# A convolutional streaming encoder layer: weight sums in the place of their first terms, a ring of five blocks, a second C22 buffer, a reordered last pair, and filler matmuls at the start

## The chip, the cores and the metric

The kernel runs on one core of a Trainium2 chip. The metric is the device time of one launch in microseconds (us). Engines are named as the profile names them: PE is TensorE (PEld its weight loads), DVE is VectorE, ACT is ScalarE, POOL is GpSimd, SP is SyncE, which here only issues transfers.

## What is computed

One layer of a chunk-causal streaming encoder on 1088 frames (1024 of a new stream, 64 of running ones), with model width 1024, DA = DB = 512 and DF = 2816. Cut to what matters:

```python
h = rms_norm(x, norm1_g)
z = h @ w_in                                   # 1024 x 4608
a_val, a_gate, b_g, c_g, b_val, gates = split(z)
u = a_val * sigmoid(a_gate)
u = silu(layer_norm(causal_dwconv31(u) + b_dw_a)) ; y_a = u @ w_a_out
v = causal_dwconv3(c_g * b_val)                   ; y_b = (b_g * v) @ w_b_out
x = x + (sigmoid(g_a) * y_a + sigmoid(g_b) * y_b) @ w_o
h = rms_norm(x, norm2_g)
f_gate, f_val = split(h @ w_up)                # 1024 x 5632
x = x + (silu(causal_dwconv3(f_gate)) * f_val) @ w_down
y = rms_norm(x, final_g)                       # and the new conv states
```

## The kernel before

**Products.** Every fp32 product is made of three matmuls in a faster number format: an operand is split into a high part and a remainder, and high x high, high x low and low x high are added (function `three`, L368 to L371). A matmul has 128 partitions and 272 columns. The two wide projections (`w_in`, `w_up`) run as a 2 x 2 scheme with seven products instead of eight. One application of it is a *job*: it makes 2 x 128 output channels for all frames (or, for half jobs, half of the frames). There are 43 jobs, j0 to j42: j0 to j5 the value and gate of mixer A (j0 to j3 are half jobs), j6 to j11 mixer B, j12 to j19 the merge gates ("S" jobs, whose results are spilled to HBM, 544 KB twice a job), j20 to j42 the up projection of the ConvFFN (j20 and j21 half jobs). Each of the seven products of a job takes one weight block of 128 x 512, and 24 matmuls (12 in a half job). In order the blocks are A11, S1, S2, S4, S3, A12, A22. A11, A12, A22 are pieces of the matrix as they are ("plain" here), and S1 to S4 are sums of pieces. Product *s* of a job is called slot *s*.

**Order on PE.** j0 to j19, then P1 (8 blocks of `w_b_out`), P2 (8 blocks of `w_a_out`), WO (32 blocks of `w_o`), j20 to j22, then ten pairs of ConvFFN channels: a job ("E"), a down projection D (4 blocks of `w_down`, 48 matmuls each), and a job ("O"). The last down projection and the transposes of the output follow. The program of each engine is written out by hand in this order.

**A block's way.** All 393 blocks are numbered. Block n comes by a transfer from SP, ACT rounds it into `w_hi` (function `hi`, L749), DVE makes the remainder `w_lo` (function `lo`, L1115), and PE uses it in product n. `w_hi` and `w_lo` have RING = 4 places, and in slot b of a job ACT and DVE handle block b + LOOK with LOOK = 3. The blocks of a job arrive in a staging tile `stg` of eight places, from which DVE makes the four sums (function `weight_sum`, L1168 to L1179) a job ahead, one in each of slots 1 to 4. Their loads wait for older blocks to be through (semaphores `wlo`, `sums`). The blocks of P1, P2, WO and D ("direct") are loaded into `w_raw`, which is the memory of `w_lo`, so their load waits until the product that used the place is done (`used`).

**Other work.** In a slot, ACT first copies results of earlier products out of the accumulator banks BA, BB, BC, BS (function `copies`), then does `hi`. DVE combines these results (the C22 half goes through `ss_w` or `ss_f`), and works on the 31 taps of mixer A's convolution (L1297, 1.38 us each, 120 of them), spread over the jobs j2 to j19. POOL adds up `e_b` over channels in three additions. After j19, DVE subtracts the mean from `cv`, and then splits `bv` into `qb_hi` and `qb_lo`, for which P1 waits. At the very end, j42 is followed by its split `q_lo`, for which the last down projection waits, since D of the pair before comes ahead of j42.

## Time and profile before

| | us |
|---|---|
| median of 3 runs (1561.3 to 1563.38) | 1561.84 |
| the profiled execution's own time | 1564.04 |
| its span | 1561.1 |
| PE busy | 1403.1 (90%) |
| DVE busy | 1111.0 (71%) |
| ACT busy | 525.4 (34%) |
| POOL busy | 79.5 (5%) |

The span is that of one profiled execution, and the times of the trace below are measured from its start. Its own time is the device time of the same execution, 2.94 us more than its span, and 2.2 us above the median. "Busy" is the time in which an engine had an instruction under way, which for PE includes stretches at the lower of its two clocks.

### The profile page before, as it was taken

Reading aid. Unit: us, or ns where it says so; the run is one execution under the profiler, and the core shown is the slowest. Engines: PE = TensorE matmul, PEld = TensorE weight load, DVE = VectorE, ACT = ScalarE, POOL = GpSimd, SP = SyncE. Lnnn points to the kernel's source line nnn. Section 1 sums busy time; section 2 is a strip of 40 time slices with the busy share of each in tenths; the row PEclk is TensorE's granted clock in tenths of the full one; section 3 lists DMA queues with packets and bytes.
Section 4 is the critical chain, followed back from the end, with each engine's and each line's share of the span. In section 5 each row is a group of like instructions: output and inputs, shape, how many; then the busy total and the mean of one; then the engine's idle time right before and its main releaser. Section 6 shows DMA issues by size and latency. Waiting matters only on the chain.

```text
span 1561.1 us, 25790 instructions
## 1 busy us (share of the span) xinstructions
PE 1403.1 (90%) x10658; PEld 1369.0 (88%) x10658; DVE 1111.0 (71%) x1622; ACT 525.4 (34%) x854; POOL 79.5 (5%) x88
## 2 busy tenths in 40 slices
PE   4799999899996899997989999999999999999967
PEld 2699999898986899986889898999999898989967
DVE  5989999998865443467776667676667766676745
ACT  6743322333433333345422222323222222223122
POOL 2000000000000042211000000000000000000001
PEclk9999999999998899988899999999999999999988
DMA  5121111122214353321111111111121111111013
GB/s 167 49 74 48 48 55 48 63 83 98 99 65 147 112 180 106 89 61 48 55 47 42 48 35 55 41 42 55 31 64 35 48 41 48 35 55 35 27 41 116
DMA packets 137659, 102.98 MB, mean 66 GB/s; under 512 B 5389, under 2 KB 130055, under 8 KB 137543
## 3 DMA queue, kind: packets, MB, share of 16 engines
q1 hardware_dynamic: 134716, 92.21, 19.5%
q10 hardware_dynamic: 2827, 9.13, 1.5%
q8 instruction: 84, 1.38, 0.4%
q14 instruction: 32, 0.26, 0.1%
HBM read 87.77 MB, written 13.55 MB: 65 GB/s over the span
## 4 chain that ended last, share of the span: by engine, by line
PE 46%; DVE 28%; issue 10%; ACT 8%; DMA 6%; POOL 1%; ACTq 0%; SPq 0%; DVEq 0%
DVE cv L1297 6%; PE BA L369 5%; PE BC L369 5%; PE BA L371 5%; PE BA L370 5%; PE BC L371 5%; PE BC L370 5%; DMA w_raw<-in_w_down 4%; DVE cvf L1532 4%; DVE w_lo L1115 4%; ACT w_hi L749 3%; PE BB L369 3%; PE BB L370 3%; PE BB L371 3%; PE BS L369 2%
## 5 line engine op out<-in xcount | busy, mean ns | idle before, releaser
L1115 DVE TENSOR_TENSOR w_lo<-stg,w_hi 128x512 fp32r<-128x512 f32 x301 | 214.4, 714 | 130.5 <-ACT w_hi L749 129.6
L749 ACT ACTIVATE w_hi<-stg 128x512 fp32r<-128x512 f32 x301 | 187.9, 626 | 292.2 <-PE BA L371 91.3
L369 PE MATMUL BB<-hb,w_hi 128*128 128x272 f32 x788 | 233.1, 296 | 35.1 <-ACT ss_f L831 22.6
L369 PE MATMUL BA<-hb,w_hi 128*128 128x272 f32 x812 | 238.7, 294 | 23.9 <-DVE t_out L1195 8.1
L370 PE MATMUL BA<-hb,w_hi 128*128 128x272 f32 x812 | 235.7, 290 | 0.0
L371 PE MATMUL BA<-hb,w_lo 128*128 128x272 f32 x812 | 235.6, 290 | 0.0
L370 PE MATMUL BB<-hb,w_hi 128*128 128x272 f32 x788 | 229.7, 291 | 0.0
L371 PE MATMUL BB<-hb,w_lo 128*128 128x272 f32 x788 | 229.2, 291 | 0.0
L369 PE MATMUL BC<-hb,w_hi 128*128 128x272 f32 x640 | 187.3, 293 | 14.6 <-ACT ss_f L822 12.4
L1115 DVE TENSOR_TENSOR w_lo<-w_raw,w_hi 128x512 fp32r<-128x512 f32 x92 | 68.2, 741 | 167.6 <-ACT w_hi L749 167.0
L369 PEld LDWEIGHTS BB<-hb,w_hi 128*128 128x128 f32 x788 | 151.6, 192 | 40.7 <-ACT ss_f L831 25.0
L370 PE MATMUL BC<-hb,w_hi 128*128 128x272 f32 x640 | 185.2, 289 | 0.0
L371 PE MATMUL BC<-hb,w_lo 128*128 128x272 f32 x640 | 185.2, 289 | 0.0
L369 PEld LDWEIGHTS BA<-hb,w_hi 128*128 128x128 f32 x812 | 155.2, 191 | 29.4 <-DVE t_out L1195 10.1
L1297 DVE SCALAR_TENSOR_TENSOR cv<-u_in,cols,cv 128x1118 f32<-128x1118 f32 x120 | 165.5, 1379 | 0.8
L371 PEld LDWEIGHTS BA<-hb,w_lo 128*128 128x128 f32 x812 | 155.4, 191 | 0.0
L370 PEld LDWEIGHTS BA<-hb,w_hi 128*128 128x128 f32 x812 | 155.2, 191 | 0.0
L370 PEld LDWEIGHTS BB<-hb,w_hi 128*128 128x128 f32 x788 | 151.5, 192 | 0.2 <-issue 0.2
L371 PEld LDWEIGHTS BB<-hb,w_lo 128*128 128x128 f32 x788 | 151.7, 193 | 0.0
L369 PEld LDWEIGHTS BC<-hb,w_hi 128*128 128x128 f32 x640 | 122.3, 191 | 17.4 <-ACT ss_f L822 14.9
L749 ACT ACTIVATE w_hi<-w_raw 128x512 fp32r<-128x512 f32 x92 | 57.9, 629 | 190.9 <-DMA w_raw<-in_w_down 96.1
L371 PEld LDWEIGHTS BC<-hb,w_lo 128*128 128x128 f32 x640 | 122.1, 191 | 0.0
(285 smaller groups left out, 3136.0 us busy)
## 6 DMA issues: line engine op xcount, KB each, us to landing
stg<-in_w_up SPq DMA_DIRECT2D x92, 256.0 KB, 3.0
stg<-in_w_in SPq DMA_DIRECT2D x80, 256.0 KB, 2.9
w_raw<-in_w_down SPq DMA_DIRECT2D x44, 256.0 KB, 2.7
gate_spill<-t_out ACTq DMA_DIRECT2D x16, 544.0 KB, 3.2
gates<-gate_spill SPq DMA_DIRECT2D x16, 544.0 KB, 4.5
w_raw<-in_w_o SPq DMA_DIRECT2D x32, 256.0 KB, 2.9
xr<-in_x_prompt SPq DMA_DIRECT2D x8, 512.0 KB, 5.8
out_y_prompt<-out_rows SPq DMA_DIRECT2D x8, 512.0 KB
```

What stands on the lines that cost most here:

```text
L369: pe.matmul(dst, w_hi[:, w, at:at + P], hi, start=first, stop=False, skip_group_check=True)
L370: pe.matmul(dst, w_hi[:, w, at:at + P], lo, start=False, stop=False, skip_group_check=True)
L371: return pe.matmul(dst, w_lo[:, w, at:at + P], hi, start=False, stop=last, skip_group_check=True)
L749: act.activation(w_hi[:, n % RING, :], src, ACT.Copy).then_inc(whi, 1)
L1115: dve.tensor_tensor(out, full, high.bitcast(F32), ALU.subtract).then_inc(done, 1)
L1297: dve.scalar_tensor_tensor(cv[c][:, :], u_in[c][:, k:k + CVW], col("dw_a", k * KA + c), cv[c][:, :], ALU.mult, ALU.add).then_inc(tap_done, 1)
L1532: dve.scalar_tensor_tensor(cvf[:, :], g_in[:, k:k + FVW], w, cvf[:, :], ALU.mult, ALU.add).then_inc(f_tap, 1)
```

## The change

**Ring and sources.** RING is 5 and LOOK is 4. Plain blocks of jobs (A11, A12, A22) are loaded straight into `w_raw` by `plain_weights`, when the place in the ring is free, like those of the other projections. `stg` has four places, one for each sum, and gets the first term of each (`first_terms`). A sum is made where its first term stands, inside `lo`, in slots 3 (one), 4 (two) and 5 (one) of the job before (`weight_sums`). The weights of a job are issued by SP in the order A11, first terms of the next job, A12, A22.

```diff
-LOOK = 3
+RING = 5
+LOOK = 4


 def streaming_encoder(nc: bass.Bass, ins, outs):
...
-                    act.wait_ge(w_in[n % RING], DIRECT[n])
+                if n in PLAIN:
+                    act.wait_ge(w_in[n % RING], PLAIN[n])
                     src = w_raw[:, n % RING, :]
...
-                        act.wait_ge(sums, 4 * j + (0, 2, 3, 4, 1)[s])
+                    j, s = SUMMED[n]
+                    act.wait_ge(wsum, 4 * j + SUM_NO[s])
+                    src = stg[:, s, :]
                 act.activation(w_hi[:, n % RING, :], src, ACT.Copy).then_inc(whi, 1)
...
+            def weight_sums(j, s):
+
+                terms = {S1: ((S1, S3),), S2: ((S3, S2), (S2, S1)), S4: ((S4, S2),), S3: ()}[s]
+                for a, b in terms:
+                    dve.wait_ge(base_in[a], 16 * (j + 1))
+                    dve.wait_ge(base_in[b], 16 * (j + 1))
+                    if a != S1:
+                        dve.wait_ge(wsum, 4 * j + SUM_NO[a] - 1)
+                    dve.tensor_tensor(stg[:, a, :], stg[:, a, :], stg[:, b, :], ALU.add).then_inc(wsum, 1)
...
+
+                if n + 1 in SUMMED:
+                    weight_sums(*SUMMED[n + 1])
                 if n >= N_END:
                     return
                 dve.wait_ge(whi, n + 1)
...
+                src = w_raw[:, n % RING, :] if n in PLAIN else stg[:, SUMMED[n][1], :]
                 sub(w_lo[:, n % RING, :], src, w_hi[:, n % RING, :], wlo)
...
+            def first_terms(j):
...
+                for s, t, c, last in ((S1, 1, c2, 3), (S2, 0, c1, 4), (S4, 1, c1, 4), (S3, 0, c2, 5)):
+                    if j == J_F:
+                        sp.wait_ge(used, N_P2)
+                    elif j:
+                        sp.wait_ge(wlo, BASE[j - 1] + last)
+                    sp.dma_start(stg[:, s, :].rearrange("p (k c) -> p k c", k=KJ),
+                                 src[:, :, t, c:c + P]).then_inc(base_in[s], 16)
+
+            def job_weights(j):
...
                 if j:
...
+                    plain_weights(BASE[j], src[:, :, 0, c1:c1 + P])
+                if j + 1 < len(JOBS) and j + 1 != J_F:
+                    first_terms(j + 1)
+                plain_weights(BASE[j] + 5, src[:, :, 1, c1:c1 + P])
+                plain_weights(BASE[j] + 6, src[:, :, 1, c2:c2 + P])

             def plain_weights(n, src):
-                sp.wait_ge(used, n - RING + 1)
+                if n >= RING:
+                    sp.wait_ge(used, n - RING + 1)
                 sp.dma_start(w_raw[:, n % RING, :].rearrange("p (k c) -> p k c", k=src.shape[1]), src).then_inc(w_in[n % RING], 16)
```

**The split of `bv` and POOL's additions.** `qb_hi` and `qb_lo` of the first two channel groups are made in slots 2 and 3 of j18 and j19, and those of the last two where all four were. The three additions into `e_b` go from POOL to DVE, into slot 0 of j19.

```diff
+            def qb_split_hi(k):
+                act.wait_ge(x_dve, X_DVE[J_S - 1])
+                if k == 1:
+                    act.wait_ge(wlo, BASE[J_F - 1] + 5)
+                elif k == 2:
+                    act.wait_ge(used, N_P1)
+                act.activation(qb_hi[k][:, :], bv[:, k, :], ACT.Copy).then_inc(qb_hid, 1)
...
+                    if j >= J_F - 2 and s == 2:
+                        qb_split_hi(j - J_F + 2)
...
-            act.wait_ge(used, N_P1)
-            act.wait_ge(x_dve, X_DVE[J_S - 1])
-            for k in range(KB):
-                act.activation(qb_hi[:, k, :], bv[:, k, :], ACT.Copy).then_inc(qb_hid, 1)
+            qb_split_hi(2)
+            qb_split_hi(3)
...
+                    if j == J_F - 1 and s == 0:
+                        dve.wait_ge(tap_done, KA * TAPS_A)
+                        dve.tensor_tensor(e_b[:, :], cv[0][:, :], cv[1][:, :], ALU.add).then_inc(e_sum, 1)
+                        for c in range(2, KA):
+                            dve.wait_ge(e_sum, c - 1)
+                            dve.tensor_tensor(e_b[:, :], e_b[:, :], cv[c][:, :], ALU.add).then_inc(e_sum, 1)
+                    if j >= J_F - 2 and s == 3:
+                        qb_split_lo(j - J_F + 2)
...
-            for k in range(KB):
-                dve.wait_ge(qb_hid, k + 1)
-                sub(qb_lo[:, k, :], bv[:, k, :], qb_hi[:, k, :], qb_lod)
+            qb_split_lo(2)
+            qb_split_lo(3)
...
-            pool.wait_ge(tap_done, 2 * TAPS_A)
-            pool.wait_ge(b_tap, 3 * KB)
-            pool.tensor_tensor(e_b[:, :], cv[0][:, :], cv[1][:, :], ALU.add).then_inc(e_sum, 1)
-            for c in range(2, KA):
```

**ConvFFN.** The C22 sums have a buffer for each parity (`ss5_f`), so that the copy in slot 2 waits for the job before the last one. In the last pair the job j42 goes ahead of D9, with `qt_hi`, `qt_lo` and `qt_raw` for the splits of the last two channel groups, and D9 and D10 stand last.

```diff
+                    elif 0 < j < J_F and JOBS[j - 1][0] != "S":
                         act.wait_ge(n2, N2[j - 1])
+                    elif j > J_F + 2:
+                        act.wait_ge(n2, N2[j - 2])
                     act.activation(ss5(j), BC[:, ps, 0:HP], ACT.Copy).then_inc(cp, 1)
...
+            for i in range(1, G - 1):
                 job(f_job(2 * i))
                 down(i - 1)
                 job(f_job(2 * i + 1))
+            job(f_job(KF - 2))
+            job(f_job(KF - 1))
+            down(G - 2)
...
+            ffn_slots(f_job(KF - 1), KF - 2, split=False)
+            for b in range(4):
+                lo(N_WD[-2] + b + LOOK)
+                for k in range(4):
+                    add_down(G - 2, 4 * b + k)
+                    if b == 0 and k < 3:
+                        f_conv(KF - 1, k)
+                    elif (b, k) == (1, 0):
+                        ffn_lo(KF - 2)
+                    elif (b, k) == (1, 3):
+                        scale_silu(KF - 1)
+                    elif (b, k) == (2, 0):
+                        value(KF - 1, 1)
+                    elif (b, k) == (2, 1):
+                        value(KF - 1, 0)
+                    elif (b, k) == (2, 3):
+                        ffn_lo(KF - 1)
```

**Beginning and middle.** PE begins with 36 matmuls of 128 columns on the identity, which nothing reads, and with 14, 5 and 5 more between the first transposes of x. The transposes of the second half of x move from slots 0 to 6 of j0 and slot 0 of j1 to slots 3 to 6 of j0 and 0 to 3 of j1, and with them the copies and block sums that they feed. Parts of the layer norm's and second RMS norm's statistics move by a product or two.

```diff
+                    if n == 0 and 1 <= t < 4:
+                        keep_busy((0, 14, 5, 5)[t])
...
+            keep_busy(36)
             turn_params()
             for k in range(KD):
                 turn_x(0, k)
-            job(0, [lambda k=k: turn_x(1, k) for k in range(7)])
-            job(1, [lambda: turn_x(1, 7)])
+            job(0, [None] * 3 + [lambda k=k: turn_x(1, k) for k in range(4)])
+            job(1, [lambda k=k: turn_x(1, k) for k in range(4, KD)])
             for j in range(2, J_F - 1):
                 job(j)
-            job(J_F - 1, [None, lambda: mean_part(0), None, None, lambda: mean_part(1)])
+            job(J_F - 1, [None, None, lambda: mean_part(0), None, lambda: mean_part(1)])
...
-                    elif h in (6, 7):
-                        ln_part(h - 6)
+                    elif h in (7, 8):
+                        ln_part(h - 7)
...
-            job(J_F, [None, None, lambda: ms_columns(1), None, None, lambda: rb_part(1)])
-            job(J_F + 1)
+            job(J_F, [None, None, None, lambda: ms_columns(1)])
+            job(J_F + 1, [None, lambda: rb_part(1)])
...
+                    if 4 <= b < 12:
+                        evac(1, b - 4)
+                    if b in (6, 8, 10, 12):
+                        blocks_b_hi(1 + b // 2)
+                    elif b in (7, 9, 11, 13):
+                        blocks_t_hi((b + 1) // 2)
...
-            for t in range(3):
+            for t in range(4):
                 x_load(t)
-            job_weights(0)
-            for t in range(3, NX):
+            first_terms(0)
+            x_load(4)
+            plain_weights(0, w_in_cols[:, :, 0, job_cols(0)[0]:job_cols(0)[0] + P])
+            for t in range(5, NX):
                 x_load(t)
-            for j in range(1, J_F):
+            for j in range(J_F):
                 job_weights(j)
```

The first place is DVE's program in slots 0 to 2 of j9, a job of mixer B. `w_lo` rows are the remainders of blocks, `bw_in` and `v_tmp` are mixer B's, `cv` rows are taps. Before:

```order
269 L1115 TENSOR_TENSOR w_lo<-stg,w_hi 128x512 [waits whi]
270 L1199 SCALAR_TENSOR_TENSOR bw_in<-BA,t_out_61 128x2x272 [waits c11,used]
271 L1236 COPY bw_in<-cols 128x2 [waits n2,x_dve]
272 L1239 COPY state<-bw_in 128x2 x2
273 L1115 TENSOR_TENSOR w_lo<-stg,w_hi 128x512 [waits whi]
274 L1251 TENSOR_SCALAR v_tmp<-bw_in,cols 128x1090 [waits b_tap,b_hist]
275 L1253 SCALAR_TENSOR_TENSOR v_tmp<-bw_in,cols,v_tmp 128x1090 [waits b_tap,b_hist]
276 L1297 SCALAR_TENSOR_TENSOR cv_70<-u_in_66,cols,cv_70 128x1118 [waits tap_done]
277 L1168 TENSOR_TENSOR stg<-stg 128x512 [waits wlo,a21_in,a11_in]
278 L1115 TENSOR_TENSOR w_lo<-stg,w_hi 128x512 [waits whi]
279 L1256 SCALAR_TENSOR_TENSOR bv<-bw_in,cols,v_tmp 128x1024 [waits b_tap,b_hist]
280 L1257 SCALAR_TENSOR_TENSOR bv<-bw_in,cols,v_tmp 128x64
```

And now, for the same job:

```order
267 L1141 TENSOR_TENSOR w_lo<-stg,w_hi 128x512 [waits whi]
268 L1214 SCALAR_TENSOR_TENSOR bw_in<-BA,t_out_61 128x2x272 [waits c11,used]
269 L1251 COPY bw_in<-cols 128x2 [waits n2,x_dve]
270 L1254 COPY state<-bw_in 128x2 x2
271 L1141 TENSOR_TENSOR w_lo<-w_raw,w_hi 128x512 [waits whi]
272 L1266 TENSOR_SCALAR v_tmp<-bw_in,cols 128x1090 [waits b_tap,b_hist]
273 L1268 SCALAR_TENSOR_TENSOR v_tmp<-bw_in,cols,v_tmp 128x1090 [waits b_tap,b_hist]
274 L1316 SCALAR_TENSOR_TENSOR cv_70<-u_in_66,cols,cv_70 128x1118 [waits tap_done]
275 L1141 TENSOR_TENSOR w_lo<-w_raw,w_hi 128x512 [waits whi]
276 L1271 SCALAR_TENSOR_TENSOR bv<-bw_in,cols,v_tmp 128x1024 [waits b_tap,b_hist]
277 L1272 SCALAR_TENSOR_TENSOR bv<-bw_in,cols,v_tmp 128x64
278 L1316 SCALAR_TENSOR_TENSOR cv_70<-u_in_66,cols,cv_70 128x1118 [waits tap_done]
```

The remainders of slots 1 and 2 (the second and third `w_lo` row) are now of blocks in `w_raw` instead of `stg`, and the sum (L1168) that stood ahead of slot 2's remainder is gone from here.

The second place is ACT's program in slots 1 to 4 of the half job j3, where `w_hi` rows are the high parts of blocks and `ss_w` rows copies out of the banks. Before:

```order
109 L749 ACTIVATE w_hi<-stg 128x512 [waits sums,used]
110 L867 ACTIVATE state<-u_in_65 128x30 [waits n2,x_dve]
111 L867 ACTIVATE state<-u_in_65 128x30
112 L822 ACTIVATE ss_w<-BC 128x272 [waits n2,used]
113 L749 ACTIVATE w_hi<-stg 128x512 [waits a12_in,used]
114 L827 ACTIVATE ss_w<-BB 128x272 [waits c22,used]
115 L749 ACTIVATE w_hi<-stg 128x512 [waits a22_in1,used]
116 L749 ACTIVATE w_hi<-stg 128x512 [waits a11_in,used]
117 L831 ACTIVATE ss_w<-BB 128x272 [waits c12,used]
118 L749 ACTIVATE w_hi<-stg 128x512 [waits sums,used]
119 L836 ACTIVATE t_out_60<-t_out_60 128x272 [waits c12]
```

And now:

```order
110 L760 ACTIVATE w_hi<-w_raw 128x512 [waits w_in1,used]
111 L880 ACTIVATE state<-u_in_65 128x30 [waits n2,x_dve]
112 L880 ACTIVATE state<-u_in_65 128x30
113 L835 ACTIVATE ss_w<-BC 128x272 [waits n2,used]
114 L760 ACTIVATE w_hi<-w_raw 128x512 [waits w_in2,used]
115 L840 ACTIVATE ss_w<-BB 128x272 [waits c22,used]
116 L760 ACTIVATE w_hi<-w_raw 128x512 [waits w_in3,used]
117 L760 ACTIVATE w_hi<-stg 128x512 [waits wsum,used]
118 L844 ACTIVATE ss_w<-BB 128x272 [waits c12,used]
119 L760 ACTIVATE w_hi<-stg 128x512 [waits wsum,used]
```

The high parts in slots 1, 2 and 3 wait for loads into the ring (`w_in`) where they waited for loads or sums in `stg`, and the copies of slots 2 and 3 stand behind them as before.

## Rows read from the trace of the kernel before

**Rows 1.** The page, part 1: busy us, share of the span, instructions.
```profile
PE 1403.1 (90%) x10658; PEld 1369.0 (88%) x10658; DVE 1111.0 (71%) x1622; ACT 525.4 (34%) x854; POOL 79.5 (5%) x88
```

**Rows 2.** Waits of PE over the span: engine, bank, line, releaser, us in total, times, longest.
```profile
PE BB L369 <- ACT ss_f L831: 22.6, 11, 2.3
PE BS L369 <- DVE q_lo L1115: 14.3, 1, 14.3
PE BC L369 <- ACT ss_f L822: 12.4, 12, 1.1
PE BS L440 <- DMA packs<-in_norm_g: 11.2, 1, 11.2
PE BS L369 <- DVE qb_lo L1115: 9.9, 1, 9.9
...
PE BB L484 <- DVE sq_b L1415: 4.7, 1, 4.7
```

**Rows 3.** Stretches: start:end, length, then busy us and instructions of each engine, granted clock, DMA.
```profile
31.90:79.30 47.40, 32.93 (x209) 28.83 (x209) 43.62 (x79) 33.37 (x59) 5.08 (x11) 1.00 0.18 51
79.30:101.40 22.10, 21.49 (x169) 21.06 (x169) 18.62 (x38) 12.55 (x29) 0.00 (x0) 1.00 0.30 85
101.40:276.00 174.60, 169.42 (x1344) 167.88 (x1344) 168.53 (x223) 55.70 (x100) 0.00 (x0) 1.00 0.18 51
276.00:442.80 166.80, 153.37 (x1177) 150.31 (x1177) 153.47 (x168) 59.94 (x102) 5.96 (x2) 0.98 0.24 80
...
782.20:1429.30 647.10, 612.52 (x4755) 603.25 (x4754) 447.13 (x703) 175.44 (x270) 0.00 (x0) 0.99 0.15 45
1429.30:1515.50 86.20, 67.81 (x530) 66.35 (x529) 56.12 (x88) 22.35 (x33) 0.00 (x0) 0.94 0.11 35
```

**Rows 4.** Timeline of j9, slots 0 to 6, and the first matmul of j10.
```profile
211.00 0.68 DVE L1115 TENSOR_TENSOR w_lo<-stg,w_hi 128x512 fp32r<-128x512 f32 x1
...
212.84 0.69 DVE L1115 TENSOR_TENSOR w_lo<-stg,w_hi 128x512 fp32r<-128x512 f32 x1 [0.18 <-ACT w_hi L749]
...
218.23 0.37 SPq L1749 DMA_DIRECT2D stg<-in_w_in  x1
...
229.53 0.72 DVE L1195 TENSOR_TENSOR t_out<-BA,t_out 128x544 f32<-128x544 f32 x1
...
230.31 0.39 PE L369 MATMUL BA<-hb,w_hi 128*128 128x272 f32 x1 [0.73 <-DVE t_out L1195]
```

**Rows 5.** Timeline of an E job, slots 4 and 5: a direct load and what follows.
```profile
1156.43 6.36 SPq L1753 DMA_DIRECT2D w_raw<-in_w_down  x3
...
1159.28 0.63 ACT L749 ACTIVATE w_hi<-w_raw 128x512 fp32r<-128x512 f32 x1 [3.09 <-DMA w_raw<-in_w_down]
...
1159.94 0.69 DVE L1115 TENSOR_TENSOR w_lo<-w_raw,w_hi 128x512 fp32r<-128x512 f32 x1 [3.16 <-ACT w_hi L749]
...
1161.75 0.69 DVE L1179 TENSOR_TENSOR stg<-stg 128x512 f32<-128x512 f32 x1
```

**Rows 6.** Timeline of the S job j17, slots 0 to 2, DVE.
```profile
402.04 0.69 DVE L1115 TENSOR_TENSOR w_lo<-stg,w_hi 128x512 fp32r<-128x512 f32 x1 [1.34 <-ACT w_hi L749]
...
404.78 0.69 DVE L1115 TENSOR_TENSOR w_lo<-stg,w_hi 128x512 fp32r<-128x512 f32 x1 [0.75 <-ACT w_hi L749]
```

**Rows 7.** Timeline of the half job j3, slots 0 to 3, ACT.
```profile
92.42 0.62 ACT L749 ACTIVATE w_hi<-stg 128x512 fp32r<-128x512 f32 x1
...
93.92 0.62 ACT L749 ACTIVATE w_hi<-stg 128x512 fp32r<-128x512 f32 x1
```

**Rows 8.** Timeline of j15, POOL and DVE side by side.
```profile
365.99 2.98 POOL L1691 TENSOR_TENSOR e_b<-e_b,cv 128x1118 f32<-128x1118 f32 x1 [73.81 <-DVE cv L1297]
366.43 3.09 DVE L1115 TENSOR_TENSOR w_lo<-stg,w_hi 128x512 fp32r<-128x512 f32 x1
```

**Rows 9.** Timeline of j0, PE, the second and third matmul.
```profile
32.30 0.43 PE L370 MATMUL BA<-hb,w_hi 128*128 128x272 f32 x1
32.52 0.43 PE L371 MATMUL BA<-hb,w_lo 128*128 128x272 f32 x1
```

284 lines of the change are left out of this document (121 added, 163 removed).

## The prediction

> **What bounds the kernel now.** I read the page first, then PE's waits, then the stretches, then the timeline of one job in each stage. PE is busy 90% of the span [rows 1]. Its work is fixed: 10368 matmuls of the three-part products at 0.125 us (12 of them in the 1.5 us of a half job's slot, [rows 7]) are 1296 us, and the change takes none away. What can move are PE's waits [rows 2] and the stretches at half clock. The stretches say who is behind the waits [rows 3]. From 101.4 to 276.0 (j4 to j11) DVE is busy 168.53 of 174.60 us, and from 276.0 to 442.8 (j12 to j18) 153.47 of 166.80: there DVE sets the pace with PE. In the ConvFFN pairs from 782.2 to 1429.3 it is busy 447.13 of 647.10, so there only short chains at a job's end count. In j9 DVE works without a gap from its remainder in slot 1 (212.84) to the bank evacuation at 229.53, for which PE waited 0.73 us before j10 at 230.31 [rows 4]. So in these jobs each microsecond that DVE is made to idle after slot 0 is a microsecond of the kernel.
>
> **What a direct load costs.** For A11, A12 and A22 the change takes the loading way of the direct blocks. Such a load is issued when a place in the ring is free, and this is at the start of the slot in which ACT already stands at that block's high part. In the E job the load is issued at 1156.43, ACT starts `w_hi` at 1159.28 and DVE `w_lo` at 1159.94, 3.5 us after the issue [rows 5]. In j9 the staged block of slot 1 had its `w_hi` ready so early that DVE waited 0.18 us [rows 4]. So a change that says "less staging, more look-ahead" puts a transfer into the path of ACT and DVE three times a job. The block itself isn't late for PE, four products ahead (12 us); DVE is, and with it the evacuations that stand behind the remainder.
>
> The Trainium skill ("DMA: Bandwidth & Descriptors", Rules for kernel authors) says to issue a transfer early, compute, and wait for its semaphore late. The new order does the opposite for these blocks; by that rule the change loses where the waiting engine has no slack, and the trace's idle times before direct blocks agree.
>
> **The change, term by term** (us, after minus before; the profiled execution's span is 1561.1, its own time 1564.04, and the median 1561.84).
>
> *j4 to j11.* In slot 1 SP must first issue S3's first term of the next job, which waits for slot 0's remainder. In j9 that remainder ends at 211.00 + 0.68 = 211.68, the issue takes 0.37 [rows 4], so A12's load starts near 212.1 and DVE can start its remainder 3.5 later, at 215.6 to 215.75, instead of 212.84: 2.9 lost. What DVE still has to do from there until PE's bank is free is the same, since all four sums were and are behind this point. That makes 2.9 for each of j7, j8, j9, which have this pattern. In j4, j5, j6, j10, j11 DVE comes to slot 1 later (0.8 to 2.7 us later in the slot than in j9 for j5, j6, j10 and j11) or has slack in places; there I take 2.6, 2.6, 1.7, 2.1 and 2.3 from the same working. Sum +20.
>
> *j12 to j18.* In j17 the remainder of slot 0 starts at 402.04, so A12's load starts near 403.1, and the remainder of slot 1 comes at 406.6, or up to 407.4 with two spills of 544 KB on the way, instead of 404.78 [rows 6]: 1.8 to 2.6 later, and ACT's copy for the next bank stands behind the same load. I take 2.4 for each of seven jobs, +17. Against it, the additions of `e_b` leave POOL. In j15 one of them (2.98) held a remainder for 3.09 [rows 8] where it takes 0.69 elsewhere. Three such, with a stretch at half clock behind the first, are -5. Net +12.
>
> The Trainium skill ("SBUF — State Buffer", Who interferes with whom) says that VectorE and GpSimd share one pair of ports as an exclusive lock, held for the whole instruction. By it the gain is 2.4 for each addition that meets a remainder; the row agrees.
>
> *j2, j3.* A product of a half job takes 1.5 us (`w_hi` at 92.42 and 93.92, [rows 7]). Three loads must each be there within the slots 1, 2 and 3, ACT's copies of the banks stand behind them, and so does PE, which needs the banks. Slot 1's load is issued 2.1 into the job and lands 5.3 into it, where ACT would have been at slot 3. Each of the two jobs takes some 14.3 instead of 11.05 (79.3 to 101.4 is 22.10 for both, [rows 3]): +6.5. Bounds: 0 if the copies are early enough, +9 if two of the loads count whole.
>
> *Beginning.* PE waits 11.2 us for the parameters, and 36 matmuls of 128 columns take about as long at low clock as this wait, so they cost 0 to 1.2. Afterwards DVE and ACT set the pace: from 31.9 to 79.3 PE is busy 32.93 of 47.40 us [rows 3]. The moved transposes thicken j1, where now normalising, block sums and direct loads meet. I take +3, bounds -4 (PE at full clock earlier, the j0 waits shorter) and +6.
>
> *j19 and the clock.* Three additions and two splits more on DVE before and in j19 cost +3. More and longer waits of PE at the jobs' ends give more stretches at half clock. The mean granted clock is 1.00 in j4 to j11, where PE waits little, 0.98 in j12 to j18 and 0.99 over the pairs [rows 3]. If the 341 us of j4 to j18 come to lose 1.5% more, this is +5 (bounds 0, +10).
>
> *P1 to WO.* Of the 9.9 that P1 waits for `qb_lo` [rows 2] 3.3 go: PE can begin with the 24 matmuls of two channel groups whose splits are made (3.0 us), and these splits are out of the way, while the mean still has to be subtracted four times before the other two. The 4.7 before the layer norm's column sums (L484, [rows 2]) go with 0.5 of half-clock time behind them, -5.2, because these now come a product later. The ring of five takes 2.5 of the small waits in WO. Sum -11, and -1 for j20 to j22.
>
> *ConvFFN, nine pairs.* An E job waits 1.03 for `ss_f` before BC and 2.05 before BB (12.4 in 12 times, 22.6 in 11, [rows 2]). The first goes with the second C22 buffer. The second gets shorter by the sum between (1161.75, pitch 0.6, [rows 5]) and 0.3 of an earlier remainder, as the sums of the O job now fall into the D phase. So E loses 1.9 of its waiting and D gets 0.9 more, from two sums ahead of one remainder. That is -9, and -2 for fewer half-clock stretches: -11 (bounds -6 and -15).
>
> *Last pair.* The 14.3 for `q_lo` [rows 2] go, since j42's and j41's splits lie under D9's 192 matmuls. j41, D9 and j42 took 86.2 [rows 3]; their 528 matmuls are 66, with the usual waits 70, and D10 gains 1.5. Sum -17.5 (bounds -20, -13).
>
> Together: 20 + 12 + 6.5 + 3 + 3 + 5 - 11 - 1 - 11 - 17.5 = +9. The same against the median gives 1571.
>
> **The rivals.** A measurement of this kernel can tell about 0.2% (3.1 us) from no change.
>
> *Faster: DVE's wait is hidden.* The 32 of j4 to j18 rest on PE having no slack against DVE there. If the ring's fourth block gives DVE the freedom to be behind without PE noticing, these 32 shrink. The point from which it decides: with less than about 1.6 us lost a full job of j4 to j18 instead of 2.5 the sum falls below -3. Hidden wholly it is 1562 + 9 - 32 = 1539; half, 1555. For it speaks that slot 1's block is ready at 213.5, three products ahead, some 6 us before its use even now; against it that PE waits for an evacuation and not for a block at 230.31 [rows 4], and no look-ahead moves that.
>
> *Much slower.* Loads that meet spills, gates and four first terms issued close together land later than 3 us, ACT's copies for the banks fall behind them also in slots 2 and 3, and the clock falls in most of these jobs. With 1 us more in each of 15 jobs and 5 more of clock: 1591.
>
> *Nothing to be seen.* The parts cancel within 3.1 us, or the fillers do what the rest loses: j0, which follows a run of transposes, still begins at half clock, one matmul each 0.22 us [rows 9], and the fillers are ordinary matmuls; but they end long before the first product, and the transposes come between. I give them nothing. The Trainium skill ("TensorE: Matmul & The Clock Gate", Part 4: PE-mode transpose) says that transposes don't count as work for the clock; by it the fillers could raise it for good and save j0 some 3 us.
>
> **How the numbers follow.** Forecast case (waits forced, 1564 to 1582) 0.55; hidden in good part (1539 to 1558) 0.27; much slower (above 1582) 0.11; cancelled (1558.7 to 1565) 0.07. From these, and with a little of the forecast case inside the 3.1 us: faster 0.28, same 0.10, slower 0.62. The predicted time is 1571. For the range I leave out the tail below 1548 and the one above 1588.
>
> **What would show it.** In the changed profile: DVE idle 2 to 3 us before the `w_lo` from `w_raw` in slot 1 of j7 to j9, with ACT's `w_hi` idle before it by the transfer; PE's waits for the evacuation (`t_out`) at these jobs' ends near 3 us instead of 0.73; j7 to j9 near 24.8 each, S jobs near 25; j2 and j3 near 14; no wait for `q_lo` before D10, and E jobs near 22.9. POOL without `e_b`. The prediction is wrong if j7 to j9 stay at 22 with DVE's idle hidden, or if the j0 and j1 stretch moves by more than 6 either way, or if the half-clock stretches change by more than 10 us in all.

## The result: 6.2% slower, and the profile after

The changed kernel takes 1659.2 us (median of 4, 1657.0 to 1661.52) against 1562.39 for the kernel before (4 runs). The ratio is 1.062, with a 95% interval from 1.0601 to 1.0639. The direction was forecast, the size was not: the loss is 97 us and not 9, and the time lies far outside the range.

First the page after: busy times, the transfers of the whole kernel, and the landing time of the spills; the transfer lines of the kernel before stand in the second fence.

```profile
PE 1449.8 (87%) x10778; PEld 1411.4 (85%) x10778; DVE 1110.6 (67%) x1625; ACT 526.6 (32%) x854; POOL 70.1 (4%) x85
DMA packets 205773, 136.82 MB, mean 82 GB/s; under 512 B 7453, under 2 KB 198167, under 8 KB 205655
...
gate_spill<-t_out ACTq DMA_DIRECT2D x16, 544.0 KB, 4.6
```

```profile
DMA packets 137659, 102.98 MB, mean 66 GB/s; under 512 B 5389, under 2 KB 130055, under 8 KB 137543
...
gate_spill<-t_out ACTq DMA_DIRECT2D x16, 544.0 KB, 3.2
```

DVE's work is the same (1110.6 us, [rows 1] has 1111.0), and its share of the longer span is lower. A spill lands in 4.6 us instead of 3.2. The transfers grew from 103.0 to 136.8 MB: a job now loads seven blocks (three plain ones and four first terms) where it loaded four, and no term of the prediction's sum counted that.

Then the stretches of the changed kernel, cut where its stages begin: start and end, length, busy us of each engine, granted clock, DMA share and GB/s.

```profile
26.10:89.50 63.40, 37.38 (x208) 32.87 (x208) 47.47 (x84) 38.63 (x68) 9.02 (x14) 0.76 0.22 63
89.50:122.20 32.70, 25.40 (x169) 24.33 (x169) 19.76 (x39) 12.63 (x30) 0.00 (x0) 0.90 0.38 107
122.20:324.30 202.10, 176.33 (x1344) 172.84 (x1344) 169.33 (x223) 55.94 (x100) 0.00 (x0) 0.97 0.26 75
324.30:523.90 199.60, 164.64 (x1176) 159.57 (x1176) 150.53 (x169) 61.44 (x102) 0.00 (x0) 0.93 0.33 97
523.90:553.40 29.50, 23.68 (x175) 22.10 (x175) 15.12 (x18) 12.72 (x21) 0.00 (x0) 1.00 0.39 123
553.40:642.90 89.50, 64.93 (x409) 61.53 (x409) 37.54 (x47) 23.86 (x30) 1.81 (x1) 0.81 0.33 106
642.90:722.80 79.90, 64.31 (x457) 62.91 (x458) 28.55 (x39) 21.91 (x32) 23.29 (x15) 0.89 0.34 105
722.80:836.10 113.30, 104.28 (x786) 103.05 (x785) 61.09 (x91) 45.57 (x75) 19.75 (x14) 0.95 0.27 79
836.10:908.00 71.90, 57.13 (x351) 54.63 (x352) 49.92 (x89) 31.34 (x55) 3.92 (x4) 0.79 0.28 80
908.00:1543.60 635.60, 606.61 (x4755) 597.29 (x4754) 444.16 (x704) 175.73 (x270) 0.00 (x0) 1.00 0.23 68
1543.60:1615.00 71.40, 68.17 (x529) 66.43 (x529) 54.74 (x88) 21.61 (x32) 0.00 (x0) 1.00 0.20 61
```

For the stages of the kernel before that [rows 3] leave out (j19, P1, P2, WO, and j20 to j22):

```profile
442.80:475.80 33.00, 23.13 (x174) 21.96 (x175) 17.34 (x19) 16.91 (x26) 3.02 (x1) 0.92 0.40 145
475.80:545.50 69.70, 60.43 (x409) 57.73 (x410) 34.17 (x44) 20.61 (x26) 1.81 (x1) 0.87 0.34 109
545.50:604.90 59.40, 56.59 (x458) 56.14 (x458) 25.35 (x38) 21.94 (x32) 26.26 (x15) 1.00 0.43 141
604.90:716.00 111.10, 104.89 (x786) 102.99 (x785) 60.16 (x91) 45.36 (x74) 19.30 (x14) 0.95 0.28 83
716.00:782.20 66.20, 52.64 (x351) 49.56 (x351) 49.71 (x89) 31.23 (x55) 3.93 (x4) 0.85 0.19 55
```

Length after minus length before, beside the terms of the prediction:

| stage | predicted | measured |
|---|---|---|
| j0, j1 with the beginning | +3 | +10.2 |
| j2, j3 | +6.5 | +10.6 |
| j4 to j11 | +20 | +27.5 |
| j12 to j18 | +12 | +32.8 |
| j19 | +3 | -3.5 |
| clock | +5 | in the other rows |
| P1, P2, WO | -11 | +19.8, +20.5, +2.2 |
| j20 to j22 | -1 | +5.7 |
| nine pairs | -11 | -11.5 |
| last pair and D10 | -17.5 | -16.0 |

So one stage, P1 and P2, went the other way and by 40 us, and j0 to j19 lost 77.6 us where 49.5 were forecast with the clock's 5. The clock column shows it too: 0.97 and 0.93 in the two long stretches of jobs, where [rows 3] have 1.00 and 0.98. The 1.00 that [rows 3] have for j0 and j1 can't be set beside the 0.76 here: until 48 us the matmuls of the kernel before stand 0.22 to 0.24 us apart, as in [rows 9], and not 0.125.

**P1 and P2: a circle through SP's queue.** What SP waited for in P1 and P2 (engine, line, releaser, us, times, longest), L1795 being the loads of gate rows:

```profile
SPq L1795 <- DVE mid L1413: 84.6, 8, 15.3
```

In the kernel before, for the same loads (its line L1763) in the same stages:

```profile
SPq L1763 <- DVE mid L1392: 16.0, 8, 6.9
```

For the products of the second merge (`mt`) it waited 32.6 us where it had waited 1.5.

The timeline of P1, in order of time, SP, ACT and DVE:

```profile
567.01 0.73 DVE L1413 TENSOR_TENSOR mid<-BA,gates 128x544 f32<-128x544 f32 x1 [2.85 <-PE BA L382]
567.76 0.32 SPq L1795 DMA_DIRECT2D gates<-gate_spill  x1
568.13 0.43 SPq L1785 DMA_DIRECT2D w_raw<-in_w_b_out  x1
572.31 0.63 ACT L760 ACTIVATE w_hi<-w_raw 128x512 fp32r<-128x512 f32 x1 [10.15 <-DMA w_raw<-in_w_b_out]
572.97 0.69 DVE L1141 TENSOR_TENSOR w_lo<-w_raw,w_hi 128x512 fp32r<-128x512 f32 x1 [5.24 <-ACT w_hi L760]
...
578.46 0.72 DVE L1413 TENSOR_TENSOR mid<-BS,gates 128x544 f32<-128x544 f32 x1
579.21 0.32 SPq L1795 DMA_DIRECT2D gates<-gate_spill  x1
```

The reader is to follow one turn. A merge (`mid`, 567.01) frees a gate row; SP loads the next one (567.76) and only then issues the next weight block (568.13). ACT can round it 4.2 us later (572.31), having been idle for 10.15, and DVE makes the remainder (572.97), having been idle for 5.24. The next merges stand behind this remainder in DVE's program, and only the second (578.46) frees the next gate row (579.21). One turn takes 11.4 us here, where two additions for the layer norm stand between the remainder and the merges, and 8.0 and 10.6 in the next two turns, for a product whose matmuls are 6 us. In the kernel before, with LOOK = 3, the weight block that DVE needs ahead of the merge of a row stood behind a gate row that waits for a merge of one row earlier, so each turn had a whole slot more.

**S jobs.** Now j17, one of the gate jobs: ACT, SP, DVE and PE.

```profile
471.43 0.88 ACTq L873 DMA_DIRECT2D gate_spill<-t_out  x2
471.49 0.37 SPq L1768 DMA_DIRECT2D stg<-in_w_in  x1
471.90 4.84 SPq L1785 DMA_DIRECT2D w_raw<-in_w_in  x3
...
478.22 0.63 ACT L760 ACTIVATE w_hi<-w_raw 128x512 fp32r<-128x512 f32 x1 [5.19 <-DMA w_raw<-in_w_in]
478.75 0.61 ACT L835 ACTIVATE ss_w<-BC 128x544 f32<-128x544 f32 x1
478.88 0.69 DVE L1141 TENSOR_TENSOR w_lo<-w_raw,w_hi 128x512 fp32r<-128x512 f32 x1 [6.12 <-ACT w_hi L760]
479.41 0.39 PE L380 MATMUL BC<-hb,w_hi 128*128 128x272 f32 x1 [3.07 <-ACT ss_w L835]
```

A12's load is issued at 471.90, right behind S3's first term and both spills (544 KB each), and ACT can start at 478.22, 6.3 us later. ACT's copy of BC (478.75) stands behind the high part, and PE waits 3.07 us for the copy. DVE has been idle for 6.12. In j9, without spills, the idle time before slot 1's remainder is 3.42 where [rows 4] have 0.18:

```profile
254.82 0.69 DVE L1141 TENSOR_TENSOR w_lo<-w_raw,w_hi 128x512 fp32r<-128x512 f32 x1 [3.42 <-ACT w_hi L760]
...
267.52 0.62 ACT L844 ACTIVATE ss_w<-BB 128x544 f32<-128x544 f32 x1 [3.93 <-DVE t_out L1206]
268.20 0.53 PE L380 MATMUL BB<-hb,w_hi 128*128 128x272 f32 x1 [2.85 <-ACT ss_w L844]
```

Its lost 3.2 us (2.9 were forecast) come back as PE's wait of 2.85 at slot 6: DVE is late with `t_out` (L1206), for which ACT's copy of BB waits, and PE waits for the copy. The fifteen matmuls behind it stand 0.23 us apart (granted clock 0.51). The wait of some 3 us for the evacuation at the job's end, which the prediction named as the sign, isn't there in j9; the lateness reached PE one bank earlier. j9 took 25.7 us instead of 21.9.

### The profile page after: what moved, and what is told of

The parts are those of the page before. It is cut to its first block, busy times and chain, and to the rows that moved or that the text cites. A ratio compares the mean times of both kernels' runs of the same rounds, so it can differ in the third digit from the quotient of the medians.

```text
span 1659.4 us, 26111 instructions
## 1 busy us (share of the span) xinstructions
PE 1449.8 (87%) x10778; PEld 1411.4 (85%) x10778; DVE 1110.6 (67%) x1625; ACT 526.6 (32%) x854; POOL 70.1 (4%) x85
## 2 busy tenths in 40 slices
DMA packets 205773, 136.82 MB, mean 82 GB/s; under 512 B 7453, under 2 KB 198167, under 8 KB 205655
## 3 DMA queue, kind: packets, MB, share of 16 engines
q1 hardware_dynamic: 202828, 126.03, 25.5%
## 4 chain that ended last, share of the span: by engine, by line
PE 45%; DVE 26%; DMA 14%; issue 7%; ACT 6%; SPq 1%; POOL 0%; DVEq 0%; ACTq 0%; POOLq 0%
DVE cv L1316 7%; DMA w_raw<-in_w_in 5%; PE BC L380 5%; PE BC L382 5%; PE BC L381 5%; PE BA L380 5%; PE BA L381 4%; PE BA L382 4%; DVE w_lo L1141 4%; PE BB L380 3%; PE BB L382 3%; PE BB L381 3%; DVE stg L1151 3%; ACT w_hi L760 3%; DMA w_raw<-in_w_up 2%
## 5 line engine op out<-in xcount | busy, mean ns | idle before, releaser
L1141 DVE TENSOR_TENSOR w_lo<-w_raw,w_hi 128x512 fp32r<-128x512 f32 x221 | 157.5, 713 | 392.2 <-ACT w_hi L760 392.1
L380 PE MATMUL BA<-hb,w_hi 128*128 128x272 f32 x812 | 241.6, 298 | 40.8 <-ACT ss_w L844 11.5
L760 ACT ACTIVATE w_hi<-w_raw 128x512 fp32r<-128x512 f32 x221 | 139.2, 630 | 424.1 <-DMA w_raw<-in_w_in 104.4
L380 PE MATMUL BC<-hb,w_hi 128*128 128x272 f32 x640 | 193.9, 303 | 39.2 <-ACT ss_w L835 32.8
L380 PEld LDWEIGHTS BA<-hb,w_hi 128*128 128x128 f32 x812 | 157.2, 194 | 46.7 <-ACT ss_w L844 13.1
L760 ACT ACTIVATE w_hi<-stg 128x512 fp32r<-128x512 f32 x172 | 106.5, 627 | 279.2 <-PE BA L382 94.9
L382 PE MATMUL BC<-hb,w_lo 128*128 128x272 f32 x640 | 190.9, 298 | 0.0
L381 PE MATMUL BC<-hb,w_hi 128*128 128x272 f32 x640 | 190.7, 298 | 0.0
L380 PEld LDWEIGHTS BC<-hb,w_hi 128*128 128x128 f32 x640 | 127.4, 199 | 43.7 <-ACT ss_w L835 35.9
L381 PEld LDWEIGHTS BA<-hb,w_hi 128*128 128x128 f32 x812 | 157.2, 194 | 0.0
L1141 DVE TENSOR_TENSOR w_lo<-stg,w_hi 128x512 fp32r<-128x512 f32 x172 | 119.1, 699 | 24.5 <-ACT w_hi L760 24.0
L382 PEld LDWEIGHTS BC<-hb,w_lo 128*128 128x128 f32 x640 | 127.6, 199 | 0.0
```

Of the source, the lines that this page charges most:

```text
L380: pe.matmul(dst, w_hi[:, w, at:at + P], hi, start=first, stop=False, skip_group_check=True)
L381: pe.matmul(dst, w_hi[:, w, at:at + P], lo, start=False, stop=False, skip_group_check=True)
L382: return pe.matmul(dst, w_lo[:, w, at:at + P], hi, start=False, stop=last, skip_group_check=True)
L760: act.activation(w_hi[:, n % RING, :], src, ACT.Copy).then_inc(whi, 1)
L1141: dve.tensor_tensor(out, full, high.bitcast(F32), ALU.subtract).then_inc(done, 1)
```

## Experiments

Each time is the median of 2 to 8 executions, compared with the kernel before on the same chip (medians 1562.96 to 1564.36 there). Stretches below are lengths between first matmuls in the one profiled execution of each kernel:

```
us                     before  after   e1     e2     e4     e3    e11     e9    e10    e12    e13    e14
j0, j1                   47.4   63.4   63.7   58.5   59.0   56.7   58.7   56.0   56.5   62.1   53.7   56.3
j2, j3                   22.1   32.7   33.6   32.5   33.4   31.5   40.0   37.7   36.2   31.1   29.6   32.0
j4 to j11               174.6  202.1  202.3  197.3  194.1  188.7  210.8  190.6  191.7  199.7  182.0  187.2
j12 to j18              166.8  199.6  199.7  204.7  185.3  194.9  199.2  180.1  182.7  196.5  182.8  177.6
P1                       69.7   89.5   69.5   61.2   88.5   63.0   89.5   63.3   61.1   87.6   63.3   62.1
P2                       59.4   79.9   59.3   57.5   79.1   57.6   79.5   57.7   57.7   80.3   57.6   57.5
WO                      111.1  113.3  110.6  102.7  112.0  102.6  111.7  102.6  102.7  113.5  102.7  102.7
nine pairs              647.1  635.6  634.8  597.7  635.2  594.8  675.2  610.4  609.9  634.8  594.9  594.9
```

**Gate rows one block later (e1).** In the changed kernel, SP's loop over the blocks of P1 and P2:

```diff
-                elif 4 <= i < 2 * KD:
-                    gate_row(i)
+                elif 5 <= i <= 2 * KD:
+                    gate_row(i - 1)
```

(the first four rows and the rows of x move by one block too).

> The changed kernel (1659), with one thing moved in SP's queue from P1 to WO: each gate row and each row block of x is issued one weight block later, so that a weight block no longer stands behind a gate row that waits for the merge of the slot before. Order theory (P1 and P2 run in a circle: gate row waits for DVE's merge, weight block stands behind it in SP's queue, ACT and DVE wait for the block, and the next merge stands behind DVE's remainder): the circle opens, P1 and P2 fall from 89.5 and 79.9 us to about 68 and 60, the whole to 1615 to 1630. Traffic theory (all transfers are late because the jobs now load 7 blocks instead of 4): P1 and P2 load nothing more than before, their blocks still land 4 us after issue, and the whole stays within 5 us of 1659.

Measured: 1619.92, ratio 1.0365 (1.0311 to 1.0419). P1 and P2 are back at 69.5 and 59.3, the values of before. P1 in its trace:

```profile
555.80:625.30 69.50, 58.95 (x408) 55.93 (x409) 38.07 (x47) 24.03 (x30) 1.81 (x1) 0.88 0.42 138
```

The circle is shown: nothing but the order of transfers in SP's queue was changed, the same bytes are moved, and 39 us are gone, within what the order theory expected (1615 to 1630). The forecast gain of 11 in P1 to WO did not come even so (69.5, 59.3, 110.6 against 69.7, 59.4, 111.1).

**Look-ahead 3 in the ring of five (e2).**

```diff
-LOOK = 4
+LOOK = 3
```

(with the fourth block taken out of the beginning and the last one put at the end by hand).

> The changed kernel with LOOK = 3 at RING = 5: one place of the ring is then spare, so a direct load is issued one slot (3 us) before ACT comes to its block, and the circle in P1 and P2 has a slot more. Same transfers, same sums, same bytes. Late-load theory (ACT and DVE stand at a block whose load has just been issued): most of the loss in j2 to j19 and in P1 and P2 goes, the whole falls to 1560 to 1600. Traffic theory: the 33.8 MB more are still moved, the whole stays above 1635.

Measured: 1546.43, ratio 0.9895 (0.9859 to 0.9931), below the lower end that the first theory had named, and 1.1% below the kernel before. The pairs:

```profile
835.30:1433.00 597.70, 596.41 (x4754) 595.32 (x4754) 443.73 (x708) 175.07 (x270) 0.00 (x0) 1.00 0.25 73
```

PE is busy 596.41 of 597.70 us in the pairs, where the change had 606.61 of 635.60 and the kernel before 612.52 of 647.10. The 113 us below the change come from P1, P2 and WO (61) and from the pairs (38). But j4 to j18 still take 402 us, as in the change, against 341 before. So the theory holds in the stages whose blocks are issued freely, and something else holds back the jobs.

**S3's first term after A12 and A22 (e4, with LOOK = 4; e3, with LOOK = 3).**

```diff
-                if j + 1 < len(JOBS) and j + 1 != J_F:
-                    first_terms(j + 1)
+                more = j + 1 < len(JOBS) and j + 1 != J_F
+                if more:
+                    first_terms(j + 1, (0, 1, 2))
                 plain_weights(BASE[j] + 5, src[:, :, 1, c1:c1 + P])
                 plain_weights(BASE[j] + 6, src[:, :, 1, c2:c2 + P])
+                if more:
+                    first_terms(j + 1, (3,))
```

> The changed kernel, with S3's first term of the next job issued after A12 and A22 instead of ahead of them. Late-load theory, as the prediction put it: A12's load is issued at the start of slot 1 instead of 0.6 us (mixer B) to 2.6 us (S jobs) later, and in the S jobs it gets ahead of part of the spills; j7 to j9 gain 0.5 each, the S jobs 2 to 3 each, j2 and j3 about 1 each; the whole 1635 to 1648. If the position does not matter (the spills delay the landing anyhow, or traffic does): 1655 to 1662.

Measured: 1630.18, ratio 1.043 (1.039 to 1.0471): 29 us less than the change, more than the 11 to 24 expected. j12 to j18 gain 14 and j4 to j11 gain 8. The place of A12's load in SP's queue counts.

> LOOK = 3 at RING = 5 and S3's first term after A12 and A22. With LOOK = 3 alone (1546) P1, P2, WO and the pairs of the ConvFFN got fast, but j4 to j11 (197 us) and j12 to j18 (205 us) did not. Late-load theory: there A12's load still stood behind S3's first term, which waits for the remainder of slot 1 now, so that the spare place brought nothing; with the order changed, j4 to j11 fall to 172 to 180, j12 to j18 to 165 to 178, j2 and j3 to 22 to 26, the whole to 1475 to 1500. Traffic theory (the jobs' seven loads land late whatever their order): j4 to j18 stay above 380 together, the whole above 1525.

Measured: 1519.75, ratio 0.9719 (0.97 to 0.9739). Faster by 27 than with LOOK = 3 alone, but neither theory's forecast: the whole is above the 1475 to 1500 of the late-load theory and below the 1525 of the traffic theory, while j4 to j18, at 384 us, stay above the 380 that the traffic theory named. The timeline of its j16, SP and ACT, shows why:

```profile
419.15 0.87 ACTq L873 DMA_DIRECT2D gate_spill<-t_out  x2
419.22 0.92 SPq L1769 DMA_DIRECT2D stg<-in_w_in  x2
420.18 2.88 SPq L1789 DMA_DIRECT2D w_raw<-in_w_in  x2
...
427.17 0.63 ACT L760 ACTIVATE w_hi<-w_raw 128x512 fp32r<-128x512 f32 x1 [4.83 <-DMA w_raw<-in_w_in]
```

A12's load (420.18) stands behind two spills and the loads of S2 and S4, all issued within 1.1 us, and lands 6.9 us later.

**Both remedies (e8).** Gate rows as in e1, on top of e3.

> As the kernel with LOOK = 3 and S3 last, and gate rows one weight block later in SP's queue too. If LOOK = 3 already opened the circle in P1 and P2 (they took 61.2 and 57.5 with it alone), this brings nothing: within 3 us of the other, and may lose 1 to 3 where a merge now waits for its gate row.

Measured: 1519.16, ratio 0.9719 (0.9695 to 0.9742): no difference from e3. LOOK = 3 had opened the circle already.

**Three loads more a job in the kernel before (e7).** Behind each of the loads of A11, A21, A12:

```diff
+                sp.dma_start(sink[3 * j + 0, :, :].rearrange("p (k c) -> p k c", k=KJ), src[:, :, 0, c1:c1 + P]).then_inc(extra, 16)
```

> The kernel before with three loads more a job (A11, A21, A12 a second time, 256 KB each, into a DRAM scratch that nothing reads), so with the changed kernel's seven transfers a job and, since the scratch is written too, more bytes than it. Output unchanged. If the traffic is what slows the changed kernel in j4 to j18: 1590 to 1640. If it only matters where something waits for a transfer just issued: before's staged loads have slack, and the whole stays within 8 us of 1563, most of that at the direct loads of P1 to D.

Measured: 1569.06, ratio 1.0049 (1.0028 to 1.0071). Seven transfers a job cost half a per cent where nothing waits for the added ones; j4 to j11 and j12 to j18 did not move (174.7, 166.8). The added transfers write to DRAM and not into the engines' memory; their packets and bytes in the trace are the change's (205773, 136.82 MB).

**Fillers alone in the kernel before (e6), and the change without them (e5).**

```diff
-            keep_busy(36)
             turn_params()
...
-                    if n == 0 and 1 <= t < 4:
-                        keep_busy((0, 14, 5, 5)[t])
```

> The kernel before with the change's 60 filler matmuls at the start and nothing else. If the fillers raise the clock for good: the first products run at 0.125 instead of 0.227 a matmul and the transposes at half their time, 3 to 6 us gained. If the transposes in between let it fall again: 0 to 1 lost, from fillers that end after the parameters have landed.

> The changed kernel without the 60 filler matmuls. If they do nothing lasting: within 3 us of 1659, j0 starting at about the same time. If they raise the clock for the first products: j0 and j1 get up to 5 us longer without them. If they delay the parameters' and the first transposes (PE busy with them when the parameters land): j0 starts 1 to 2 us earlier and the whole is 1 to 3 us shorter.

Measured: e6 1562.96, ratio 0.9992 (0.9977 to 1.0007). e5 1655.58, ratio 1.0593 (1.0536 to 1.065), an interval that overlaps the change's. The fillers do nothing that can be measured in the time. They do change the clock, though. Five transposes of x in the kernel before (line L459), five in e6 (L464), and the first product of e6:

```profile
23.01 1.36 PE L459 MATMUL BA<-ident,x_tile 128*128 128x128 f32 x5
...
22.00 0.83 PE L464 MATMUL BA<-ident,x_tile 128*128 128x128 f32 x5
31.59 0.59 PE L369 MATMUL BA<-hb,w_hi 128*128 128x272 f32 x1 [6.48 <-ACT hn_w L775]
```

Behind the fillers five transposes take 0.83 us where they took 1.36. PE then waits 6.48 us for ACT's `hn_w` where it had waited 3.7, and after this wait the granted clock is 0.50 (31.6 to 39.0), so that j0 begins at half clock as before. In e6 the first product begins at 31.6 us where it began at 31.9, and j0 and j1 take 47.7 where they took 47.4. In e5 it begins at 28.1 where the change has 26.1, and j0 and j1 take 62.5 for 63.4.

**All first terms after A12 and A22 (e9 and e10 with LOOK = 3, e11 with LOOK = 4).**

```diff
-                if j + 1 < len(JOBS) and j + 1 != J_F:
-                    first_terms(j + 1)
                 plain_weights(BASE[j] + 5, src[:, :, 1, c1:c1 + P])
                 plain_weights(BASE[j] + 6, src[:, :, 1, c2:c2 + P])
+                if j + 1 < len(JOBS) and j + 1 != J_F:
+                    first_terms(j + 1)
```

> LOOK = 3 at RING = 5, and all four first terms of the next job issued after A12 and A22. With only S3 moved (1520), j4 to j18 were still 37 us... that is 384 us against 341 before. In its S jobs A12's load is issued at 420.18, right behind the two spills (419.15, 419.57) and the loads of S2 and S4, and lands 6.9 us later. Queueing theory (a load lands late when it is issued behind the spills and behind loads that nobody needs yet): now A12 is issued at the start of slot 1, ahead of the spills, and lands in 3 to 4; j12 to j18 fall from 195 to 165 to 178, j4 to j11 to 174 to 182, the whole to 1485 to 1505. Rival (the spills' 1.1 MB delay any load of this slot, whatever its place): j12 to j18 stay above 188, the whole above 1510.

Measured: 1535.47, ratio 0.9829 (0.9807 to 0.9851). j12 to j18 fell to 180.1, just above the 165 to 178 expected, but j4 to j11 rose to 190.6 where 174 to 182 were expected, and the whole, above the 1485 to 1505 expected, got slower than e3. In j17:

```profile
443.89 3.37 SPq L1785 DMA_DIRECT2D w_raw<-in_w_in  x2
...
444.34 0.81 ACTq L873 DMA_DIRECT2D gate_spill<-t_out  x2
...
447.41 0.62 ACT L760 ACTIVATE w_hi<-w_raw 128x512 fp32r<-128x512 f32 x1
```

A12's load, issued at 443.89 ahead of the spills, is there when ACT comes to it at 447.41, without any idle time. So the rival, that the spills delay any load of this slot, is refuted for a load issued ahead of them. But the four first terms then go out in one piece behind A22, and the next load into the ring stands behind them; j2 and j3 (37.7) and the pairs (610.4) got longer.

> The changed kernel (RING 5, LOOK 4) with only SP's order inside a job changed: all first terms after A12 and A22. It parts the two causes in j4 to j18: the load's place in the queue, and the spare place in the ring. With S3 alone moved j4 to j11 took 194 and j12 to j18 185. Both-causes theory: j4 to j18 take 370 to 380, as each direct load is still issued when ACT stands at it (3 us), but not more; P1 and P2 stay near 88 and 79; the whole 1622 to 1632. If the queue's place were all, j4 to j18 would fall to 345 to 355.

Measured: 1720.46, ratio 1.101 (1.0973 to 1.1046), a clear miss: I had expected a gain. With a look-ahead of four A11's load has no slack at all, and now four first terms go out just ahead of it. In a job of the pairs:

```profile
1126.85 2.15 SPq L1768 DMA_DIRECT2D stg<-in_w_up  x4
1129.44 0.37 SPq L1785 DMA_DIRECT2D w_raw<-in_w_up  x1
...
1134.20 0.63 ACT L760 ACTIVATE w_hi<-w_raw 128x512 fp32r<-128x512 f32 x1 [3.66 <-DMA w_raw<-in_w_up]
```

ACT can start 4.8 us after the issue, having been idle for 3.66. Against e4, where one first term stands there, the pairs take 40 us more (675.2), j4 to j11 17 and j12 to j18 14. Which load stands behind which matters more than how many there are.

**The beginning as before (e10).** On top of e9, the transposes of x, copies, block sums and norms in the old slots.

```diff
-            job(0, [None] * 3 + [lambda k=k: turn_x(1, k) for k in range(4)])
-            job(1, [lambda k=k: turn_x(1, k) for k in range(4, KD)])
+            job(0, [lambda k=k: turn_x(1, k) for k in range(7)])
+            job(1, [lambda: turn_x(1, 7)])
```

> The kernel with the first terms last, and the beginning as before the change: transposes of the second half of x, copies, block sums and norms in the slots of the old order (fillers stay). If the moved transposes are what made j0 and j1 longer (63.4 instead of 47.4 in the change, 57 with LOOK = 3), they fall to 45 to 50 and the whole is 5 to 10 us shorter than the kernel with the first terms last. If the direct loads of the first jobs made them longer, j0 and j1 stay above 54.

Measured: 1542.0, ratio 0.9879 (0.9854 to 0.9904), 6.5 slower than e9. j0 and j1 stay at 56.5, and the first product begins at 31.4 instead of 26.2. So the new order of the beginning gains 5 us, and does not make j0 and j1 longer. That leaves the direct loads and the sums in them; these two were not parted.

**The bytes of the first terms taken away (e12 with LOOK = 4, e13 in e3).** Here the first terms of all jobs but j0 and j20 load 4 of their 128 columns a piece, so that the sums are made of old data; every wait, issue and order stays.

```diff
+                    w = P if j in (0, J_F) else 4
-                    sp.dma_start(stg[:, s, :].rearrange("p (k c) -> p k c", k=KJ),
-                                 src[:, :, t, c:c + P]).then_inc(base_in[s], 16)
+                    sp.dma_start(stg[:, s, :].rearrange("p (k c) -> p k c", k=KJ)[:, :, 0:w],
+                                 src[:, :, t, c:c + w]).then_inc(base_in[s], 16)
```

> The changed kernel (LOOK 4), in which the first terms of all jobs but j0 and j20 are loaded in only 4 of their 128 columns a piece (8 KB instead of 256 KB), so that the sums are made of old data; every wait, issue and order stays. It takes the bytes away and leaves the issue at the wrong moment. Late-issue theory: j4 to j11, where a load lands 3 to 3.5 us after issue without company, stay at 192 to 202; the S jobs, whose A12 landed after 6.2 behind first terms and spills, gain 1 to 2 each, to 185 to 192; the pairs don't change (635); the whole 1630 to 1650. Traffic theory: j4 to j18 come back to 350 or less together, and the whole to 1600 or less.

Measured: 1644.77, ratio 1.0514 (1.0484 to 1.0544), 14 us less than the change. j4 to j11 and j12 to j18 fall by 2.4 and 3.1 only, the latter less than the 8 to 15 that the late-issue theory expected. A12's load in j17, as above:

```profile
464.38 4.84 SPq L1786 DMA_DIRECT2D w_raw<-in_w_in  x3
...
470.21 0.63 ACT L760 ACTIVATE w_hi<-w_raw 128x512 fp32r<-128x512 f32 x1 [4.71 <-DMA w_raw<-in_w_in]
```

ACT can start 5.8 us after the issue, where it was 6.3: what the load stands behind is mostly the two spills. At LOOK = 4 the bytes of the first terms are a small part; the moment of issue is the large one.

> The same cut of the first terms' bytes in the kernel with LOOK = 3 and S3 last (1520). There a load has one slot of time. If what it still loses against the kernel before in j2 to j18 (315 us against 363 to 366... that is 415 against 363 in all) is loads that queue behind one another and land after 5 to 7 us, then j12 to j18 fall from 195 to 168 to 182 and j4 to j11 from 189 to 176 to 185, the whole to 1480 to 1505. If it is the order of the sums on DVE (three of four in slots 5 and 6), nothing changes by more than 5 us.

Measured: 1495.93, ratio 0.9563 (0.9537 to 0.9589), as expected for loads that queue. With a slot of time for each load, what is left depends on it in part: j4 to j11 fall from 188.7 to 182.0, j12 to j18 from 194.9 to 182.8. The rest to 174.6 and 166.8 is not the first terms' bytes. What it is stays open; the sums' later slots and the remaining loads behind the spills are the candidates. One reservation on both: the small loads still are as many packets (205773).

**The better order for each kind of job (e14).**

```diff
+                early = (0,) if j > J_S and j < J_F else (0, 1, 2)
                 if more:
-                    first_terms(j + 1, (0, 1, 2))
+                    first_terms(j + 1, early)
```

(and the others after A22).

> LOOK = 3 at RING = 5, with the better order of loads for each kind of job: in j13 to j19, where the spills are, S1 ahead of A12 and A22 and the other three behind; elsewhere S1, S2, S4 ahead and S3 behind. From the two kernels' stretches (j2 and j3 31.5, j4 to j11 188.7, j12 to j18 180.1 or less, pairs 594.8) the whole should be 1500 to 1508. If the orders act on each other (the first terms arrive too late for the sums in slot 4): 1510 to 1525.

Measured: 1499.25 (4 runs, 1496.84 to 1501.4), ratio 0.9579 (0.9554 to 0.9604). The remedies add up, and the kernel is 4.2% faster than the one before, 160 us below the change as made. j4 to j11 take 187.2 us, j12 to j18 177.6, and in the pairs PE is busy for 594.90 of 594.90 us. The jobs j4 to j18 are still 23 us above the kernel before.

## Why the prediction was wrong

**Right, with the mechanism.** Direct loads put a transfer into ACT's and DVE's path, and a look-ahead of the ring's size less one does not hide it: the 3.42 us of idle time in j9 and PE's wait behind it show it, though PE's wait came by ACT's copy and not by the evacuation that the prediction named. The last pair with D10 (-16.0 for -17.5) came as worked out. The nine pairs (-11.5 for -11) have the right total with some luck: E fell by 2.6 us a pair (from 25.5 to 22.9) and D rose by 1.3 (from 25.4 to 26.8), where 1.9 and 0.9 were forecast, with 2 us in all for the clock. And e2 and e3 show 38 to 41 us more in the pairs that the late loads hold back, which no term saw. The half jobs (+10.6 for +6.5, bounds 0 to 9) had the right mechanism, and a size just above the bound. That the fillers gain nothing is confirmed by e6, but not that the transposes undo them: they raise the clock for the transposes, and it is down again when j0 begins, behind a wait for ACT.

**Wrong in sign: "The ring of five takes 2.5 of the small waits in WO. Sum -11".** This is the step that cost most. I read P1 to WO from PE's waits and did not walk SP's queue there, although the longer look-ahead moves each of its weight blocks against the gate rows: with LOOK = 4 the block that DVE needs before it can merge row m stood in the queue behind a gate row that can be loaded only after the merge of row m - 1. e1 undoes just this, and gets 39 us back. Instead of -11, P1 to WO had +42.5. Even without the circle, in e1, 0.8 of the 11 appeared at LOOK = 4. PE's wait for `sq_b` stayed, 4.2 us for the 4.7 of [rows 2]:

```profile
PE BS L380 <- DVE qb_lo L1141: 4.5, 1, 4.5
...
PE BB L504 <- DVE sq_b L1436: 4.2, 1, 4.2
```

The wait for `qb_lo` fell from 9.9 to 4.5. At LOOK = 3 P1 and WO do fall, by 6 to 9 each, so the gain belongs to the place of the ring that is spare.

**Mis-sized: "or up to 407.4 with two spills of 544 KB on the way".** DVE's remainder comes 7.0 us after the issue of A12's load (471.90 to 478.88), not 3.5 to 4.3 as taken (403.1 to 406.6 or 407.4), and DVE lost 5.4 in slot 1 of an S job (idle 6.12 against 0.75 in [rows 6]) instead of 1.8 to 2.6. The net +12 of j12 to j18 was +32.8: j12, in which nothing is spilled yet, lost 0.6, and the six others 3.2 to 6.8 each. The row with spills and a waiting load at once was not in the trace of before, since there nothing waited for a load in these slots; I should have bounded it by the bytes ahead in the queue. e9 shows the position's part, as A12 lands in 3.4 us ahead of the spills.

**Mis-sized: j0 and j1 (+3, bounds -4 and +6).** They took 63.4 us instead of 47.4; with the earlier beginning this is +10.2. The prediction had named a move of more than 6 in this stretch as a sign that it is wrong. e10 clears the moved transposes of it; the rest stays open.

**Mis-sized: the clock (+5, bounds 0 and 10).** By the granted clock of the stretches, j4 to j18 have 3% of 202.1 and 7% of 199.6 us missing, 20 us against 3 in [rows 3]; some of this is in waits and costs nothing. It is inside the measured +27.5 and +32.8, and was not parted from them. This too was named as a sign of being wrong (more than 10 us).

**Missed: bytes and packets.** The change moves 33.8 MB more. e7 and e12 put it at 0.5 to 0.9%, less than where the loads stand; the packets, which e12 leaves, were not parted from the bytes.

**Not tried.** What the additions of `e_b` cost on POOL and on DVE was not measured alone. The -5 for it can't be told from the rest of j12 to j18; j19, where I put +3 for them, got shorter by 3.5.

By the rule on transfers that the prediction named (the Trainium skill, "DMA: Bandwidth & Descriptors", Rules for kernel authors: issue early, wait late) the change had to lose where it now issues late. The runs agree: at RING = 5 the same kernel takes 1659 with a load issued in the slot in which it is awaited, and 1546 with one slot between.

The rival "hidden" is refuted, and "much slower" was right in kind (loads behind spills and first terms), with a price that was four times too small: 20 us above the forecast, and 88 were measured, of which the circle in P1 and P2, which it did not have, is 39.

## What to carry to other kernels

A look-ahead as long as the ring less one leaves a direct load no time: it is issued when its reader already stands there. One place of slack (ring five, look-ahead three) was worth 113 us here. When a look-ahead is changed, walk every queue that carries other transfers between the blocks, and ask for each block which wait now stands ahead of it; a circle through queue, reader and the work behind the reader shows in the trace as one idle time that comes again (DVE's 5.24, 5.26 and 5.21 us before three remainders of P1) and as waits of the queue for the work behind the reader (84.6 us for 16.0). Where some transfers are awaited and others are not, the awaited ones go first.

## What the runs showed of the hardware

A 256 KB load into the ring, which took 2.9 us (median) in the ConvFFN's jobs, took 6.2 us in j17 behind two transfers of 544 KB and one of 256 KB from two queues, issued within half a microsecond, and 6.9 in e3 with one more of 256 KB ahead; issued 0.45 us ahead of the two large ones, in e9, it took 3.4. Sixty matmuls of 128 columns, 36 of them before the transposes and 24 between, brought five later transposes from 1.36 to 0.83 us and left nothing measurable in the time (0.9992, 0.9977 to 1.0007). Cutting four loads a job from 256 KB to 8 KB, at an equal number of packets, gave 14 us of 1659.
